# Prompt queries of a latent-attention layer: one product per head, or pairs of heads with the rotated part made at once and carried over DRAM

## The reference

```python
z = rmsnorm(h, ln_in) @ w_in                 # c_q (256), c_kv (128), k_r (32), g_a, u_val, u_gate, g_c
q = (rmsnorm(c_q, ln_q) @ w_q_b).reshape(b, t, N_HEADS_A, QK_NOPE + QK_ROPE)   # 8 heads of 64 + 32
q_nope, q_rope = q[..., :QK_NOPE], rope(q[..., QK_NOPE:], pos)
ckv_new, kr_new = rmsnorm(c_kv, ln_kv), rope(k_r[:, :, None, :], pos)[:, :, 0, :]
# scores of a head: (q_nope . keys(ckv)) + (q_rope . kr), softmax over earlier chunks of 64 frames
```

## Time and profile before

| | us |
|---|---|
| median of 3 runs (lowest to highest) | 790.71 (790.63 to 790.83) |
| the profiled execution | 791.15 |
| its span | 789.4 |
| matmuls busy | 765.8 |
| weight loads busy | 606.3 |
| VectorE busy | 561.5 |
| ScalarE busy | 425.2 |
| POOL busy | 65.0 |

### The profile page before, as it was taken

One profiled execution on the slowest core, in us unless ns is written; L12 is line 12 of the kernel. 1 busy time (PEld: TensorE's weight loads), 2 busy tenths in 40 slices (PEclk: granted clock), 3 DMA queues, 4 the chain that ended last, 5 costly groups with the idle time before them and its releaser, 6 DMA issues.

```text
span 789.4 us, 10538 instructions
## 1 busy us (share of the span) xinstructions
PE 765.8 (97%) x3767; PEld 606.3 (77%) x3767; DVE 561.5 (71%) x1086; ACT 425.2 (54%) x982; POOL 65.0 (8%) x114
## 2 busy tenths in 40 slices
PE   8999999999998999999999999999999899999995
PEld 7799877677766588888888988776777666888874
DVE  3449989877765995646463799897778579656477
ACT  3765656764455653353365484657545558223654
POOL 1400123200000500000000011222000000000000
PEclk9999999999999999999999999999999999999998
DMA  8822222100000354422182323121000004341203
GB/s 269 248 76 81 81 70 84 38 28 27 1 27 1 105 175 145 113 78 81 54 271 58 102 75 91 49 58 28 27 27 28 1 27 139 115 146 54 83 25 134
DMA packets 45833, 65.54 MB, mean 83 GB/s; under 512 B 12590, under 2 KB 24714, under 8 KB 45766
## 3 DMA queue, kind: packets, MB, share of 16 engines
q1 hardware_dynamic: 41946, 58.45, 23.7%
q0 software_dynamic: 3776, 6.40, 2.7%
q10 hardware_dynamic: 60, 0.02, 0.0%
HBM read 57.87 MB, written 7.18 MB: 82 GB/s over the span
## 4 chain that ended last, share of the span: by engine, by line
PE 86%; DVE 7%; ACT 6%; issue 1%; POOL 0%; ACTq 0%; DVEq 0%; POOLq 0%
PE acc L653 19%; PE acc L659 19%; PE acc L656 19%; PE acc L789 4%; PE sharedT L581 4%; PE sharedS L864 4%; PE sharedO L878 3%; PE sharedT L851 3%; PE sharedO L581 2%; PE sharedS L581 2%; PE sharedS L837 1%; PE sharedS L838 1%; DVE VT L1532 1%; PE sharedO L825 1%; ACT KH L1044 1%
## 5 line engine op out<-in xcount | busy, mean ns | idle before, releaser
L653 PE MATMUL acc<-WHI,XHI 128*128 128x512 f32 (+1 forms) x710 | 309.2, 435 | 0.9 <-ACT WHI L1044 0.4
L659 PE MATMUL acc<-WHI,XLO 128*128 128x512 f32 (+1 forms) x710 | 274.8, 387 | 0.0
L656 PE MATMUL acc<-WLO,XHI 128*128 128x512 f32 (+1 forms) x710 | 274.3, 386 | 0.3 <-DVE WLO L1462 0.3
L1532 DVE SCALAR_TENSOR_TENSOR VT<-UX,CWT,VT 128x640 f32<-128x640 f32 x240 | 211.5, 883 | 4.9
L653 PEld LDWEIGHTS acc<-WHI,XHI 128*128 128x128 f32 x710 | 133.8, 188 | 32.8 <-issue 8.7
L656 PEld LDWEIGHTS acc<-WLO,XHI 128*128 128x128 f32 x710 | 134.0, 189 | 30.6 <-issue 8.1
L1462 DVE SCALAR_TENSOR_TENSOR WLO<-WR,GT,WHI 128x512 fp32r<-128x512 f32 (+1 forms) x142 | 98.7, 737 | 79.7 <-ACT WHI L1044 79.0
L659 PEld LDWEIGHTS acc<-WHI,XLO 128*128 128x128 f32 x710 | 133.3, 188 | 26.0
L1044 ACT ACTIVATE WHI<-WR,GT 128x512 fp32r<-128x512 f32 (+1 forms) x142 | 93.4, 709 | 91.2 <-PE acc L659 91.0
L1260 ACT ACTIVATE SB<-SB,NBIAS 128x384 f32<-128x384 f32 (+1 forms) x80 | 45.9, 574 | 47.7 <-DVE NBIAS L1586 47.1
L1044 ACT ACTIVATE PT<-sharedT 128x384 f32<-128x384 f32 (+1 forms) x80 | 35.4, 443 | 45.5 <-PE sharedT L581 45.0
(11 more groups left out here) (200 smaller groups left out, 864.0 us busy)
## 6 DMA issues: line engine op xcount, KB each, us to landing
WR<-in_w_in_dram SPq DMA_DIRECT2D x32, 256.0 KB, 3.0
WR<-in_w_in_dram SPq DMA_DIRECT2D x16, 512.0 KB, 3.7
WR<-in_w_out_dram SPq DMA_DIRECT2D x16, 512.0 KB, 3.6
WR<-in_w_pg_dram SPq DMA_DIRECT2D x16, 512.0 KB, 3.5
H<-in_x_prompt_dram SPq DMA_DIRECT2D x16, 256.0 KB, 4.9
WR<-in_w_in_dram SPq DMA_DIRECT2D x8, 416.0 KB, 3.8
residual_spill<-H SPq DMA_DIRECT2D x5, 512.0 KB, 4.1
H<-residual_spill SPq DMA_DIRECT2D x10, 256.0 KB, 3.4
```

The source lines that it names most:

```text
L653: mm(out, hi, w_hi, start=(first and k == 0), stop=False)
L656: mm(out, hi, w_lo, start=False, stop=False)
L659: last = mm(out, lo, w_hi, start=False, stop=(final and k == 1))
L1532: stt(out=out, in0=src, scalar=w, in1=out, op0=ALU.mult, op1=ALU.add).then_inc(conv_done, 1)
```

## The change

Per layer and core, the change does this.

- **Prompt queries.** `WQ` is laid out by pairs of heads, 256 columns each: rotated part of the even head and its exchange, unrotated parts of both heads, rotated part of the odd head and its exchange. `queries(h)` is called for even `h` and makes the unrotated parts of two heads (bank T; for head 0 bank S as before).
- **Rotated parts.** ScalarE gathers the 16-wide first halves of all heads into one 128-column weight (`WQR`), the second halves into another. `rotated_queries` multiplies both in samples' steps 2 and 3; VectorE makes the four products with cosine and sine (`COS8`, `SIN8`, tables loaded by SP) into `OTOK`. The four products of each head go to DRAM as 64 rows; the scores' contraction over these 64 rows with the rotated key adds them up. POOL writes `q_spill` with eight DMAs, waits for them, and reads one head's rows into `QH[64:128]` for each head: head 0 at once, heads 1 and 2 after the last samples' scores, the others when the scores of the third head before are done. `QH` has three slots.
- **Copies.** `queries_out(0)` is two VectorE copies. For the later pairs of queries and of keys ScalarE copies the first head (384 columns, then the last 128 behind a wait for VectorE) and VectorE the second.
- **Filler.** Samples' steps have 3 halves each (before 4, the last two 3), units 1, 2, 2, 1 (before 1, 1, 2, 1); of step 0's halves two stand before the loop. Taps and splits are placed anew. `filler_gate` works on the unit before and stands ahead of the last taps; ScalarE's `block_out("prep")` is new.
- **Banks.** The second value rows (`("v", 1)`) move from S to O; `("qr", 0)` and `("qr", 1)` lie in O.
- **Start.** In layer 0 one weight step of `u0` (part 2, tile 0) moves ahead of the turn of the convolution's state.

The diff, cut:

```diff
-for _n, _m in [*enumerate([4, 4, 4, 4, 4, 4, 3, 3]), ("prep", 4), *((NB + u, (1, 1, 2, 1)[u % 4]) for u in range(UNITS))]:
+for _n, _m in [*enumerate([3] * NB), ("prep", 4), *((NB + u, (1, 2, 2, 1)[u % 4]) for u in range(UNITS))]:
...
-for _u in (5, 13, 21):
+for _u in (1, 8, 14, 21):
     del SPLIT_AT[NB + _u]
-for _n, _u in enumerate((2, 10, 18)):
+for _n, _u in enumerate((6, 10, 18)):
...
-    TAP[_n] = _take((4, 4, 5, 4, 5, 4, 4, 4)[_n])
+    TAP[_n] = _take((4, 4, 3, 3, 5, 4, 4, 4)[_n])
...
-for _u, _m in enumerate((1, 1, 1, 3, 1, 1, 2, 2, 1, 1, 1, 3, 1, 1, 3, 2, 1, 1, 1, 3, 1, 1, 1, 1, 2, 1, 1, 2)):
+for _u, _m in enumerate((1, 2, 2, 2, 1, 2, 2, 2, 1, 2, 1, 2, 1, 2, 3, 1, 1, 2, 1, 2, 1, 2, 3, 1, 0, 2, 1, 1)):
...
         def load_wq(eng, l):
             for k in range(2):
-                eng.dma_start(WQ[:, k, :, 0:NOPE + ROPE],
-                              a["w_q_b"][l, P * k:P * (k + 1), :].rearrange("p (h e) -> p h e", h=HEADS)).then_inc(wq_in, 16)
+                src = a["w_q_b"][l, P * k:P * (k + 1), :].rearrange("p (g x e) -> p x g e", g=HEADS // 2, x=2)
+                eng.dma_start(WQ[:, k, :, 128:224], src[:, 1]).then_inc(wq_in, 16)
+                eng.dma_start(WQ[:, k, :, 64:128], src[:, 0, :, 0:NOPE]).then_inc(wq_in, 16)
+                eng.dma_start(WQ[:, k, :, 0:ROPE], src[:, 0, :, NOPE:]).then_inc(wq_in, 16)
...
+                if j == first_j + RAW + 2:
+                    copied_wait(sp, (l, "p2"))
+                    for x, row in ((COS8, NOPE), (SIN8, P - 16)):
+                        src = a["c_ropet"][row:row + 16, 0:SEQ].unsqueeze(0).to_broadcast([HEADS, 16, SEQ])
+                        sp.dma_start(x, src).then_inc(rope8_in, 16)
...
+                if l == 0:
+                    copied_wait(pe, (l, ("x", 0, 1)))
+                    quantum("u0", 2, 0)
...
-                    last = mm(bank((l, name))[:, :], WQ[:, k, h, :], CQT[:, k, 0:SEQ], start=(k == 0), stop=(k == 1))
+                    last = mm(bank((l, name))[:, :], WQ[:, k, h // 2, 64:192], CQT[:, k, 0:SEQ],
+                              start=(k == 0), stop=(k == 1))
...
+            def rotated_queries(half):
+                name = ("qr", half)
+                fill_wait(pe, (l, name))
+                pe.wait_ge(wqr_ready, 4 * (l + 1))
+                for k in range(2):
+                    w = WQR[:, k, half].rearrange("p g x e -> p (g x e)")
+                    last = mm(bank((l, name))[:, :], w, CQT[:, k, 0:SEQ], start=(k == 0), stop=(k == 1))
+                fill_inc(last, (l, name))
...
-                    copied_wait(pe, (l, ("q", h)))
+                    copied_wait(pe, (l, ("q", h - h % 2)))
+                    pe.wait_ge(q_rot_in[h % 3], 16 * (h // 3 + 1 + (3, 3, 2)[h % 3] * l))
...
-            filler(0, slice(0, 1))
+            filler(0, slice(0, 2))
...
+            for k in range(2):
+                for half in range(2):
+                    copy(WQR[:, k, half], halves[:, k, :, :, 16 * half:16 * (half + 1)]).then_inc(wqr_ready, 1)
...
+            def queries_out(h):
+                name = ("q", h)
+                filled_wait(act, (l, name))
+                copy(QH[0:NOPE, h % 3, 0:384], bank((l, name))[0:NOPE, 0:384])
+                act.wait_ge(q_second, (HEADS // 2 - 1) * l + h // 2)
+                drain_inc(copy(QH[0:NOPE, h % 3, 384:512], bank((l, name))[0:NOPE, 384:512]), (l, name))
...
             probs_out(NB, 1)
+            block_out("prep")
...
-                drain_inc(tt(QH[:, h % 2, :], bank((l, name))[:, :], ROPET[:, 0:SEQ], ALU.mult), (l, name))
+                for a in range(2):
+                    out = nc.vector.tensor_copy(QH[0:NOPE, h + a, :], bank((l, name))[NOPE * a:NOPE * (a + 1), :])
+                drain_inc(out, (l, name))
+            def second_queries_out(h):
+                name = ("q", h)
+                filled_wait(dve, (l, name))
+                nc.vector.tensor_copy(QH[0:NOPE, (h + 1) % 3, :], bank((l, name))[NOPE:P, :]).then_inc(q_second, 1)
+            def rotate_queries(half):
+                name = ("qr", half)
+                if half == 0:
+                    dve.wait_ge(rope8_in, 32 * (l + 1))
+                filled_wait(dve, (l, name))
+                x = bank((l, name))[:, :]
+                tt(QROT[half], x, COS8, ALU.mult).then_inc(q_rotated, 1)
+                if half == 0:
+                    drain_inc(tt(QROT[3], x, SIN8, ALU.mult), (l, name))
+                else:
+                    drain_inc(stt(out=QROT[2], in0=x, scalar=-1.0, in1=SIN8, op0=ALU.mult, op1=ALU.mult), (l, name))
...
-                if i == 2 and h < HEADS - 1:
-                    queries_out(h + 1)
+                if i == 3 and h in (0, 2, 4):
+                    second_keys_out(h + 2)
+                if i == 2 and h in (1, 3, 5):
+                    second_queries_out(h + 1)
+                filler_gate(NB + u - 1 if u else "prep")
                 taps(TAP.get(NB + u, [])[early:])
-                filler_gate(NB + u)
...
+            def rotated(h):
+                pool.dma_start(QH[NOPE:P, h % 3, :], q_spill[h].rearrange("x j n -> (x j) n")).then_inc(q_rot_in[h % 3], 16)
+            for half in range(2):
+                copied_wait(pool, (l, ("qr", half)))
+            pool.wait_ge(q_rotated, 2 * (l + 1))
+            for h in range(HEADS):
+                pool.dma_start(q_spill[h].rearrange("x j n -> j x n"), OTOK[NS * h:NS * (h + 1), 0:4, :]).then_inc(q_spilled, 16)
+            pool.wait_ge(q_spilled, 16 * HEADS * (l + 1))
+            rotated(0)
+            filled_wait(pool, (l, ("s", NB - 1)))
+            rotated(1)
+            rotated(2)
...
+            for h in range(3, HEADS):
+                filled_wait(pool, (l, ("s", NB + 4 * (h - 3) + 3)))
+                rotated(h)
```

More of the change, by code:

```diff
@@ L250, in build @@
         KRB = SB[:, 1, 0:32 * TILES].rearrange("p (t a e) -> p t a e", t=TILES, a=2)
+        COS8, SIN8 = QH[:, 0, :], OTOK[:, 4, :]
+        QROT = [OTOK[:, x, :] for x in range(4)]
         NBIAS = sb("NBIAS", [P, NB + UNITS])
@@ L322, in build @@
         rope_copied = sem("rope_copied")
+        rope8_in = sem("rope8_in")
+        q_second = sem("q_second")
+        q_rotated = sem("q_rotated")
+        q_spilled = sem("q_spilled")
+        q_rot_in = [sem(f"q_rot_in{slot}") for slot in range(3)]
+        k_second = sem("k_second")
         lnf_in = sem("lnf_in")
@@ L715, in tensor_layer @@
             for c in (2, 3):
-                for t in range(TILES):
+                for t in range(1 if (l, c) == (0, 2) else 0, TILES):
                     copied_wait(pe, (l, ("x", t, 1)))
@@ L744, in sample_queries @@
                     for k in range(2):
-                        last = mm(quad(name)[:, j, :], WQ[:, k, 4 * g + j, :], CQT[:, k, SEQ:TOK],
+                        w = WQ[:, k, 2 * g + j // 2, P * (j % 2):P * (j % 2 + 1)]
+                        last = mm(quad(name)[:, j, :], w, CQT[:, k, SEQ:TOK],
                                   start=(k == 0), stop=(k == 1))
@@ L1345, in scalar_layer @@
                     value_rows_out(3)
+                if i == 2 and h in (1, 3, 5):
+                    queries_out(h + 1)
                 if i == 3 and h in (0, 2, 4):
@@ L1571, in vector_layer @@
                 filled_wait(dve, (l, name))
-                rope = ROPET[:, SEQ:TOK].rearrange("p (s t) -> p s t", t=NS)
-                for j in range(4):
-                    out = tt(QS[:, :, 4 * g + j, :], quad(name)[:, j, :].rearrange("p (s t) -> p s t", t=NS),
-                             rope, ALU.mult)
-                drain_inc(out, (l, name))
+                heads = QS.rearrange("p s (g x) t -> p x g s t", x=2)
+                rope = ROPET.rearrange("p a (s t) -> p a s t", t=NS).unsqueeze(2).to_broadcast([P, 2, 2, NB, NS])
+                new = bank((l, name))[:, :].rearrange("p (g x s t) -> p x g s t", x=2, s=NB, t=NS)
+                at = slice(2 * g, 2 * g + 2)
+                nc.vector.tensor_copy(heads[0:NOPE, 0, at], new[NOPE:P, 0])
+                tt(heads[NOPE:P, 0, at], new[0:NOPE, 0], rope[0:NOPE, 1], ALU.mult)
+                drain_inc(tt(heads[:, 1, at], new[:, 1], rope[:, 0], ALU.mult), (l, name))
             low(first_i + 12)
@@ L1618, in vector_layer @@
                     sample_mask(s + 1)
-                    taps(s)
+                    if s in (2, 3):
+                        taps(TAP[s][:2])
+                        rotate_queries(s - 2)
+                        taps(TAP[s][2:])
+                    else:
+                        taps(s)
                 else:
@@ L1625, in vector_layer, with second_keys_out @@
                 filler_gate(s)
+            def second_keys_out(h):
+                name = ("k", h)
+                filled_wait(dve, (l, name))
+                nc.vector.tensor_copy(KH[0:NOPE, (h + 1) % 3, :], bank((l, name))[NOPE:P, :]).then_inc(k_second, 1)
             def head_out(h):
```

52 lines of the change are left out of this document (34 added, 18 removed).

## The result

The changed kernel took 785.9 us (median of 5 runs, 785.75 to 787.84) beside 790.83 us of the kernel before (5 runs, 790.63 to 791.18): ratio 0.9943, interval 0.9929 to 0.9958. It is faster by 4.9 us, inside the range of 774.5 to 786.5, but the forecast was 10.0 us. So the question is where 5 us went.

The account below looks back on a forecast made before the run. TensorE, busy for 765.8 of 789.4 us, was taken as the bound. Terms -6.9 - 12.1 + 9.0 = -10.0 us took the profiled 791.15 to 781.15, or 780.7 us as median; range 774.5 to 786.5.

Parts of the forecast that it names:

- the rival of VectorE in the heads: Masks come late in four units a layer, so VectorE becomes the bound in the heads: 786 us, chance 0.14.
- Costed at nothing: Weight copies, query-weight and table loads, VectorE's rotated products and extra matmuls in the samples' stage: hidden or offset, 0 us.
- Part 1: Prompt queries: 12 matmuls of 512 columns for 16 a layer, eight fewer in two layers at 0.86 us, -6.9 us.
- Part 2: TensorE's named waits on other engines in both layers go, 7.1 us of them for VectorE's masks: -12.1 us.
- V, CTK and KH: Waits expected to go: value rows' shared bank 1.4 us, second sample's scores 0.9, ScalarE's copies of both heads' keys 1.1.
- Part 3: New TensorE waits in samples' stage and heads, 4.5 us a layer: +9.0 us.
- first PT: First sample step: TensorE reaches the values sooner and waits for ScalarE's probabilities, +1.4 us a layer.
- queries: First prompt scores: two VectorE copies from PSUM, 1.2 us, replace the rotated product, +0.4 us a layer.
- the start of the heads: Second unit waits because two gate tiles follow the first unit's probabilities on ScalarE, with VectorE's mask behind: +1.6 us a layer.
- so that stage keeps its length: Samples' stage: two extra pairs of matmuls (3.4 us) replace six halves (4.1), so its length stays the same.
- Part 4: Rotated rows' writes to DRAM and first reload finish by 152, scores need them at 158: hidden by 6 us, cost 0.
- Late rotated rows: Eight DRAM writes finish one after another, so first scores wait 10.9 us in each layer: 802 us, chance 0.07.

Follow-up runs that it names:

- first: Against the changed kernel, ScalarE instead of VectorE copies the even heads' unrotated sample queries; 783.9 us, ratio 0.9915.
- second edit: Against the changed kernel, one filler half goes ahead of the rotated queries' matmuls in samples' steps 2 and 3; 785.94 us, ratio 0.9937.
- all five edits: Changed kernel plus ScalarE sample-query copy, half before rotated queries, 5, 3, 2, 2, 3... halves, earlier first late-gate tile, earlier small cache loads; 777.62 us, ratio 0.9831.

## Why the prediction was half right

The measured 785.9 us lies in the range by luck: it is near the upper end, which stands there for the rival of VectorE in the heads, and the forecast's own steps give 780.7. The step that failed is *"Costed at nothing"*, the fourth point below.

- *Part 1, matmuls, -6.9.* Right: 6.93 by the run that puts them back. TensorE's busy time fell by less, 4.0 us, because other places gained some.
- *Part 2, waits that go, -12.1.* Right. None of these waits is left at its place. Of the start the trace shows the wait come back, while the time (0.8 for 0.9) is within the spread of the runs. The gate's move was shown alone; it is worth more than the 7.1 us, 13.0 in the changed kernel, as new gates hang on it. V, CTK and KH were not tried alone; their rows are gone.
- *Part 3, new waits, +9.0.* Near, 4.2 us a layer for 4.5: first PT 1.1 for 1.4, queries 0.66 for 0.4, the start of the heads 0.97 + 0.27 + 0.51 = 1.75 for 1.6, pinches 0.4 for 0.3, last head 0.25 for 0.8. The queries' copies are the two of 0.69 us that the prediction took from the product's row:

```profile
157.18 1.39 DVE L1687 COPY QH<-sharedS 64x512 f32<-64x512 f32 x2 [2.27 <-PE sharedS L884]
```

  The Trainium skill, VectorE: DVE Perf Modes (Why PSUM operands drop a tier), has fp32 copies out of PSUM at single speed; the trace agrees, 0.69 us for 512 columns. VectorE waited for the matmul before them, 2.27 us where it was 1.78 before the change, so it was their own length that TensorE waited for.
- *"Costed at nothing"* is the step that failed, in two ways. It left out an operation: the samples' query output was never listed among the edits, and costs 0.86 us of VectorE a layer where VectorE has next to no slack; 1.9 us in the timelines, 2.0 in the run that gives it to ScalarE. And *"so that stage keeps its length"* counted only TensorE's own instructions. Per layer the stage also got two waits for bank O (0.31 each), and in layer 1 the wait for a cache. POOL starts to ask for the fifth sample's cache when the first one's values are done:

```profile
121.72 0.77 POOL L509 DMA_DIRECT2D V<-in_cache_ckv_dram  x1 [12.11 <-PE sharedO L859]
122.49 1.46 POOL L513 DMA_DIRECT2D CKR<-in_cache_krope_dram  x2
```

  The last of these is issued at 123.23 and lands 2.4 us later, at 125.66 (the median of all these loads is 2.4 us too). TensorE turns this cache from 126.09 on, and first waits for all its loads. Before, the last load landed at 125.58, and with one half more in that step the turn came at 126.75. So 1.2 us of cover became 0.4. That is too little when a load is slow: in the profiled runs of the first and second edit this one took 3.7 us and TensorE waited 0.8. In layer 1 the load is no slower, but POOL is late:

```profile
505.75 0.78 POOL L509 DMA_DIRECT2D V<-in_cache_ckv_dram  x1 [13.19 <-issue]
509.55 0.41 PE L609 MATMUL sharedT<-IDENT,V 128*128 128x128 f32 x2 [0.47 <-DMA CKR<-in_cache_krope_dram]
```

  It issues 1.50 us after the end of the first sample's values, where it is 0.29 in layer 0 and in both layers before, and for the 1.2 us more the profile names nothing that it waited for. The same 1.2 us stand in layer 1 of seven of the nine single experiments, but not in the one with more writes nor in the one with the loads moved ahead, so that last one took away two things at once. By this the load lands at 509.41 and not at about 508.2, and TensorE, which by layer 0's starts is ready at 508.91, waits. What holds POOL up stays open. Together, bank O and the cache are the 0.6 and 0.9 us more per layer.
- *Part 4, over DRAM, 0.* Right, with its 6 us of margin. A write lands in 3.2 us, close to the 3.0 of the row taken. The Trainium skill, DMA: Bandwidth & Descriptors (Anatomy of one DMA, SWDGE path), gives an estimate of 2.3 us by its fit: the reload's 2.4 agrees; the write's 3.2 is longer, and the page warns of long receipts when the target is HBM.
- *The rivals.* VectorE did become the bound, at another place than the heads, so its 786 us was met by luck, for a reason that this rival did not name. Late rotated rows did not happen; its price from the point where it decides would have been higher than worked out, by the clock.

The 0.3 us between embedding and next queries are a wait as well. Ahead of layer 1's samples' queries ScalarE stands still for 0.37 us between two of its own operations, VectorE's split comes later for it, and TensorE's weight load waits 0.31 us for WLO at 464.71:

```profile
455.28 0.42 ACT L1087 ACTIVATE JUNK<-Z 128x256 bf16<-128x256 f32 x1 [0.37 <-ACT JUNK L1087]
```

The pause is in neither the kernel before nor the two with the first edit, whose stretch is 219.6 us again, and it is in all the others. Why it comes is not shown, and 0.4 us a layer in the heads stay open.

## What to carry to other kernels

Go through the diff operation by operation and give each one a row, also those that only follow from a new layout: an output that splits the partitions in two costs the engine twice, and whether that is free is read from the engine's busy share in its own stretch, not over the layer. When work is thinned out on the bounding engine, ask of every transfer with a fixed distance of steps whether the shorter step is still longer than issue plus landing, and count the landing from the start of the issue. Where the gains sit at different waits of one path, they add; test each alone and then all, since one may hide behind another, as the rotated product's place did behind the caches.

## What the runs showed of the hardware

- One wait of 5 us on TensorE costs more than itself: behind 4.95 us the granted clock was 0.50, the lower of its two levels (1.2 and 2.4 GHz), for over 5 us, and the stretch to the embedding was 2.8 us longer in layer 0. Behind waits of 1.1 us, and of 2.5 us in the run with the gates put back, it stayed at 1.00. The Trainium skill, TensorE: Matmul & The Clock Gate (HAM oscillation), says that a wait for a transfer can throttle the array so that the work behind it starts at half speed; the trace agrees.
- VectorE's time went by columns, not rows: 0.42 us for 64x256 and for 128x256.
- Twenty-four writes of 128 KB issued 0.51 us apart landed later and later, at first 2.8 us behind their issue and at last 6.3: 6.11 us from the last issue to the last receipt, for 3.53 with eight.
- TensorE's busy time is no count of its work: a wait in the weight loads can lie under the record of the matmul before. It fell by 0.8 us where only the rotated products moved, by 2.8 us (761.8 to 759.0) with all five edits, and no matmul was taken away.
